# Scores of the dilated groups: three float32r products of high and low parts in place of one native float32 matmul

## The reference

```
qc = partial_rope(qc...); kc = partial_rope(kc...)
for gi, (window, dil) in enumerate(C_PATTERNS):
    half = (window // 2) // dil
    o, lse = banded_attention(fold(q[:, :, gi], dil), fold(k[:, :, gi], dil), fold(v[:, :, gi], dil), half)
    ...
w = softmax(stack(lses)); o = sum(w[..., None] * stack(outs))

# in banded_attention
sc = einsum("nbqhgd,nbkhd->nbhgqk", q_blk, k_blk) * (dh ** -0.5)
sc = where(valid, sc, NEG_INF); lse = logsumexp(sc); p = exp(sc - lse); o = einsum(p, v_blk)
```

## Time and profile before

| | |
|---|---|
| median of three runs | 1225.15 us (1224.0 to 1225.29) |
| span of the profiled execution | 1220.5 us |
| the rest of an execution, by the median of the runs (the page gives the span alone) | 4.65 us |
| TensorE busy with matmuls | 1202.9 us, 99% |
| VectorE, ScalarE busy | 704.6 us (58%), 560.0 us (46%) |
| the chain that ended last, by engine | TensorE 95%, DMA 3%, VectorE 1% |

### The profile page before, as it was taken

The page is one execution under the profiler, slowest core; times in us unless marked ns, Lnnn a source line. Parts: engine busy times, 40 slices in busy tenths (PEclk is TensorE's granted clock), DMA queues, the critical chain, the costliest instruction groups (busy, mean ns, idle before and its releaser), DMA issues.

```text
span 1220.5 us, 15416 instructions
## 1 busy us (share of the span) xinstructions
PE 1202.9 (99%) x5756; PEld 1001.2 (82%) x5756; DVE 704.6 (58%) x844; ACT 560.0 (46%) x730; POOL 72.9 (6%) x128
## 2 busy tenths in 40 slices
PE   7999999999999999999999999999999999999997
PEld 5788888888888888788888888888888888888886
DVE  5475555465565855763555545465655556667654
ACT  5544443454454634564434444434344444445442
POOL 2400001001000000010000000001000001000000
PEclk9999999999999999999999999999999999999999
DMA  9995453545434455355344454544534455334441
GB/s 361 258 304 183 143 199 140 174 145 226 164 152 159 173 185 203 142 207 198 147 175 170 154 189 158 187 172 172 194 152 172 176 202 207 138 139 172 179 167 69
DMA packets 33436, 219.90 MB, mean 180 GB/s; under 512 B 4288, under 2 KB 4416, under 8 KB 7920
## 3 DMA queue, kind: packets, MB, share of 16 engines
q1 hardware_dynamic: 30672, 209.73, 47.6%
q0 software_dynamic: 1856, 7.38, 2.4%
q10 hardware_dynamic: 864, 2.18, 0.5%
HBM read 217.17 MB, written 2.10 MB: 180 GB/s over the span
## 4 chain that ended last, share of the span: by engine, by line
PE 95%; DMA 3%; DVE 1%; ACT 0%; SPq 0%; issue 0%; ACTq 0%; DVEq 0%
PE acc L379 85%; PE bank_x L530 2%; DMA probs<-x_nat 2%; PE bank_x L514 1%; PE bank_y L483 1%; DMA raw<-weights 1%; PE bank_x L459 1%; PE bank_y L459 1%; PE bank_x L499 1%; PE bank_y L499 1%; PE bank_y L477 1%; PE bank_x L526 1%; PE bank_x L416 0%; PE bank_y L416 0%; DVE w_lo L888 0%; ACT w_hi L636 0%
## 5 line engine op out<-in xcount | busy, mean ns | idle before, releaser
L379 PE MATMUL acc<-w_hi,act_hi 128*128 128x512 f32 x1560 | 622.0, 399 | 2.6 <-DVE w_lo L888 2.6
L379 PE MATMUL acc<-w_lo,act_hi 128*128 128x512 f32 x1560 | 609.5, 391 | 0.0
L888 DVE TENSOR_TENSOR w_lo<-raw,w_hi 128x2048 fp32r<-128x2048 f32 x195 | 447.4, 2294 | 208.2 <-ACT w_hi L636 208.0
L636 ACT ACTIVATE w_hi<-raw 128x2048 fp32r<-128x2048 f32 x195 | 373.6, 1916 | 244.6 <-PE acc L379 219.0
L379 PE MATMUL acc<-w_hi,act_lo 128*128 128x512 f32 x1560 | 418.4, 390 | 0.1
L379 PEld LDWEIGHTS acc<-w_hi,act_hi 128*128 128x128 f32 x1560 | 293.5, 188 | 62.2 <-DVE w_lo L888 2.3
L379 PEld LDWEIGHTS acc<-w_hi,act_lo 128*128 128x128 f32 x1560 | 293.1, 188 | 62.7 <-DVE act_lo L897 0.7
L379 PEld LDWEIGHTS acc<-w_lo,act_hi 128*128 128x128 f32 x1560 | 293.9, 188 | 56.8
L643 ACT ACTIVATE unit<-acc,pre_r 128x512 f32<-128x512 f32 x78 | 49.3, 684 | 116.2 <-PE acc L379 115.7
L658 ACT ACTIVATE probs<-scores,negm 128x256 f32<-128x256 f32 (+1 forms) x80 | 36.7, 459 | 125.0 <-DVE negm L968 99.6
L332 POOL TENSOR_TENSOR rope_c<-unit,cst 128x256 f32<-128x256 f32 (+1 forms) x19 | 15.1, 797 | 924.5 <-ACT unit L643 924.5
(11 more groups left out here) (171 smaller groups left out, 611.0 us busy)
## 6 DMA issues: line engine op xcount, KB each, us to landing
raw<-weights SPq DMA_DIRECT2D x195, 1024.0 KB, 4.8
resid<-x_turned SPq DMA_DIRECT2D x8, 256.0 KB, 10.0
mix<-rpb POOLq DMA_DIRECT2D x32, 64.0 KB, 24.4
postg<-post_g POOLq DMA_DIRECT2D x2, 1024.0 KB, 23.5
resid<-x_perm POOLq DMA_DIRECT2D x2, 1024.0 KB, 6.5
out<-resid SPq DMA_DIRECT2D x8, 256.0 KB, 2.5
raw<-weights SPq DMA_DIRECT2D x2, 512.0 KB, 5.6
postg<-x_nat ACTq DMA_DIRECT2D x2, 512.0 KB, 9.6
```

Of the source, the lines that this page charges most:

```text
L379: m = nc.tensor.matmul(tiles[t][:, :], a[:, kt, t * P:(t + 1) * P], w[:, buf, kk * NB:(kk + 1) * NB], start=(kt == 0 and a is act_hi and w ...
L636: nc.scalar.activation(w_hi[:, at % SPLIT, :], raw[:, at % RAW, :], ACT.Copy).then_inc(S["hi_ready"], 1)
L888: nc.vector.tensor_tensor(w_lo[:, at % SPLIT, :], raw[:, at % RAW, :], w_hi[:, at % SPLIT, :].bitcast(F32), ALU.subtract).then_inc(S["lo_r ...
```

## The change

G's q and k are taken apart into `qT_hi`, `qT_lo`, `kT_hi` and `kT_lo` like those of the other units, and G's scores go through the same loop over `PARTS`, with the 128 keys of the query's own tile. The two views of `postg` are gone, and GpSimd's DMA into `postg` waits for another, earlier event.

```diff
-        g_qT, g_kT = postg[:, 0:UH * SEQ], postg[:, UH * SEQ:]
-
...
         def qk_parts(u, f):
 
-            if u.kind == "G" or u.kind == "D" and f in (2, 3):
+            if u.kind == "D" and f in (2, 3):
                 return None
...
-            pool.wait_ge(S["masked"], UH * 8)
+            pool.wait_ge(x_new[1], OUT_BLOCKS)
             pool.dma_start(postg[:, :], post_g[1].partition_broadcast(P)).then_inc(S["postg_in"], 16)
...
                     mine = slice(j % UH * SEQ + t * P, j % UH * SEQ + (t + 1) * P)
-                    if u.kind == "G":
-
-                        m = nc.tensor.matmul(Y[:, cols], g_qT[:, mine], g_kT[:, keys], start=True, stop=True)
-                        continue
...
                 if parts is None:
-                    tile = unit_out_flat if u.kind == "D" else (g_qT, g_kT)[f // 2]
 
                     dve.wait_ge(S["qk_full"], 4 * u.index + f + 1)
-                    nc.vector.tensor_copy(tile[:, f % 2 * NB:(f % 2 + 1) * NB], bank[f % 2][:, :]).then_inc(
+                    nc.vector.tensor_copy(unit_out_flat[:, f % 2 * NB:(f % 2 + 1) * NB], bank[f % 2][:, :]).then_inc(
                         S["qk_ready"], 1)
                     return
                 hi, lo, n = parts
 
-                before = 4 * u.index if u.kind != "D" else 4 * (u.index - 4)
-                dve.wait_ge(S["qk_hi"], before + (3 if f == 4 else f + 1))
+                dve.wait_ge(S["qk_hi"], 4 * u.index + (3 if f == 4 else f + 1))
```

## The result

The change made the kernel slower, by a third of a percent: nine runs of each gave medians of 1227.23 us after and 1222.9 us before, and the ratio of the two is 1.0033 with a 95% interval of 1.0023 to 1.0043. That is some 4.0 us by ratio (2.8 to 5.3); forecast were 3.6. The nine runs of before include the three that the prediction had, of 1224.0 to 1225.29; the other six took 1222.09 to 1224.07. So the median of before came out 2 us lower than the prediction's, and the ratio, not the time, is the number to read.

The account below looks back on a forecast made before the run. TensorE was taken to bound the kernel, busy 1202.9 of 1220.5 us. Per G score 0.675 us added less 0.45 removed, by 16 scores, gave 1225.15 + 3.6 = 1228.8 us; range 1227.9 to 1229.6, 8 in 10 1226.0 to 1239.6.

Parts of the forecast that it names:

- native score, removed: On TensorE, each G score's four native matmul records go away, taking off 0.45 us a score.
- step of a float32r product with 128 columns: On TensorE in G's scores, each new product takes 0.1125 us, between 0.108 and 0.118.
- the score after: On TensorE, a G score of six float32r products takes 0.675 us.
- the load sets it, not the stream: In G's products, loading the stationary operand (107 ns) sets the step, not streaming 128 columns (53 ns).
- fills on ScalarE and VectorE: In G's fills, ScalarE's 16 added copies (9.5 us) and VectorE's subtractions cost the end 0.
- slack of the first score: In each G unit, the last low part is done about 1.05 us before the first score starts.
- GpSimd's DMA: The DMA into postg stays behind the last rotary step despite its new wait: 0.
- G units in all: Over the four G units, 16 scores at +0.225 us each add 3.6 us.
- Rival A: In G's products the stream sets the step, up to one a 64 ns: 1224.1 us; chance 0.14 with cases between.
- The gain worked out from them: On TensorE, three float32r passes for four native ones would win 1.8 us over G's 16 scores.
- Rival B: G's short float32r products lose their single pass: +13.2 to +14.4 us, 1238.4 to 1239.6 us; chance 0.25.
- Rival C: TensorE waits for the low parts at the first score of each G unit: 1232.8 us; chance 0.04.

Follow-up runs that it names:

- the late low part: The changed kernel with two idle ScalarE copies of 1024 elements ahead of fill 3's high part in each G unit; G stretch 283.85 us.
- the old wait: The changed kernel with GpSimd's earlier wait put back ahead of its DMA into postg; G stretch 281.25 us.

## Why the prediction was right

| step of the prediction | forecast | measured |
|---|---|---|
| native score, removed | 0.45 us | 0.45, by the kernel with native scores and the new fills (0.01 us off in the stretch) |
| step of a float32r product with 128 columns | 0.1125 us (0.108 to 0.118) | 0.112, from two products to three |
| the score after | 0.675 us | 0.67 in the timeline |
| the load sets it, not the stream | argued from durations | shown: within 4 ns from 64 to 256 moving columns; 0.06 with 64 stationary columns |
| fills on ScalarE and VectorE | 0 | 0.01 us in 277 |
| slack of the first score | about 1.05 us | 1.06 between the rows; 1.77 us of delay cost 0.87 a unit, so some 0.9 |
| GpSimd's DMA | 0 | 0.01 us |
| G units in all | +3.6 us | +4.16 us |
| time of the whole | 1228.8 us, +3.6 | 1227.23 us, +4.0 by ratio (2.8 to 5.3) |

The time itself came out below the 1228.8, and below the forecast's own range of 1227.9 to 1229.6 (by its sum 1225.15 + 4.1 + 0.5 the upper end is 1229.75), because before ran faster than in the prediction's three runs; it lies inside the range that holds 8 in 10. The agreement of 1227.23 with the forecast is thus worth less than that of the growth: that came out a little above. The mechanism is the one forecast, and the experiments show it apart from the number.

**The term that was too small** is the sum over the scores, 16 x 0.225 = 3.6 against 16 x 0.26. The steps inside the score were right; the prediction put the projection behind it at no change, and there some 0.035 us a score come on top. In after and then in before, a row of the half chunk behind the first score:

```profile
745.97 0.39 PE L377 MATMUL acc<-w_hi,act_hi 128*128 128x512 f32 x1
```

```profile
746.73 0.39 PE L379 MATMUL acc<-w_hi,act_hi 128*128 128x512 f32 x1
```

It is the eleventh projection matmul behind the second one. The eleven steps take 745.97 - 743.43 = 2.54 us, against 746.73 - 744.23 = 2.50, and the difference is there within the first nine of them. With two products this extra is 0 at the first head of a unit and some 0.04 at the other three, where native matmuls with v stand directly ahead of the score. It is not ScalarE's or VectorE's doing, for it is gone with native scores on the same fill path. What makes it was not settled: the number of loads in a row doesn't, since before had eight in a row at those three heads (four with v, four of the score) without it. Timing has a part: with the late low part it is 0, 0, 0.04 and 0.01 us behind the first scores of the four units, whose instructions are the same. The cause stays open.

**Rival A** (the stream sets the step) fell with the experiments on 64 columns and on two products; the inference from 190 against 139 ns of load was the one that held. The figure of the page "TensorE: Matmul & The Clock Gate" of the Trainium skill (Back-to-back issue gap), 81 ns a pair at 128 columns, doesn't describe float32r operands here: 112 ns measured. The same page of the Trainium skill, in its section on LDWEIGHTS, gives columns / 1.2 ns, 107 ns for 128 and 53 for 64; this case's steps of 0.11 and 0.06 us agree. The four passes of native float32 in "FP8 and Floating Point Precision" of the Trainium skill (TensorE Precision Notes) fit what streams here: a native record of 128 columns that doesn't wait for its load lasts 270 ns (the minimum) and a float32r one 220, some 50 ns more, one pass, and two such records make four. The gain worked out from them didn't come, because that count leaves out the loads. **Rival B** (a quarter of the rate) fell too: it asked for 213 to 225 ns a product, and the steps are 0.11 us, 0.06 with 64 stationary columns. The argument that the prediction had against it was weaker than it says: from 512 to 256 columns the duration falls from 390 to 283 ns, by a pass, but not in proportion, and the 283 hold a wait for the load. **Rival C** didn't occur, and its margin was measured: some 0.9 us in place of the 1.05 read.

## What to carry to other kernels

A float32 matmul taken apart into three float32r products trades two records, each with a stream of two passes, for three with one pass. With 128 moving columns each record costs the load of its stationary operand, so count the loads: 6 x 0.112 here against 4 x 0.112. With 256 the native record's stream counts and the three are cheaper: a W score takes 0.71 us, and a native score with 256 columns, of D's late heads in before, takes 1061.04 - 0.23 - 1059.94 = 0.87:

```profile
1059.94 1.03 PE L480 MATMUL bank_y<-late_k,unit_out 128*128 128x256 f32 x4
...
1061.04 0.40 PE L379 MATMUL acc<-w_lo,act_hi 128*128 128x512 f32 x1
```

If the parts are needed for their precision, let one loaded part meet both parts of the other operand in one matmul of twice the columns and add the halves on an idle engine (0.46 us in place of 0.67).

To measure a change of 0.3% with such a spread of runs, take the distance between two starts of the bound engine that enclose the change: here it agreed to 0.01 us between kernels that do the same on that engine, while whole executions of one kernel differed by 2 to 5 us.

## What had not been expected of the hardware

A matmul's shown duration holds its wait for the stationary operand: 220 ns for the first float32r product of a unit's first score, 272 to 281 for the ones that follow it, and 191 or 192 and then 275 to 278 with 64 columns. Behind the matmuls with v, where the first product waits too, it lasts 304 to 306. The 512-column matmuls behind a float32r score can take 4 ns more each for about nine of them, open as said. Two products in a row with the same stationary operand, as hi x hi and hi x lo here, each show a load and pay for it (0.11 us), until one matmul takes both. And the stretch of 277 us, with DMA traffic and three engines beside TensorE, came out the same to 0.01 us in the two pairs of kernels that give TensorE the same work there: before and native scores on the new fill path (277.08 and 277.09), after and the old wait (281.24 and 281.25).
